# Seven norms of a two-block transformer taken token tile by token tile, with the first gate and up chunks computed in rows and turned

## The reference

```python
# first block, for l in 0, 1
h = rmsnorm(x, norm_mix_g[l])
q, k, v, f_logit, cx, cb, cc, px, gate_logit = split(h @ w_in[l])
merged = g0 * attention(q, k, v, f) @ w_attn_out + g1 * conv(cx, cb, cc) @ w_conv_out + g2 * pooling(px)
x = x + merged @ w_o[l]
h = rmsnorm(x, norm_ffn_g[l])
gt, up = split(h @ w_ffn_in[l])
x = x + (silu(gt) * up) @ w_ffn_out[l]
# second block, for i in 0, 1
h = rms_norm(x, norm_mix[i]) * (1 + scale1) + shift1
x = x + gate1 * mixer_i(h)          # i = 0: latent attention, i = 1: dilated attention
h = rms_norm(x, norm_mlp[i]) * (1 + scale2) + shift2
x = x + gate2 * (square(relu(h @ mlp_w1[i])) @ mlp_w2[i])
```

## Time and profile before

| | us |
|---|---|
| median of 3 runs | 1592.36 |
| lowest, highest | 1590.96, 1592.88 |
| profiled execution, its own time | 1587.97 |
| its span | 1586.2 |
| TensorE busy | 1539.4 (97%) |
| its weight load busy | 1391.3 (88%) |
| VectorE busy | 1126.1 (71%) |
| ScalarE busy | 819.1 (52%) |
| GpSimd busy | 132.5 (8%) |

### The profile page before, as it was taken

How to read it: one execution, slowest core, us unless ns; L and a number is a source line. 1 busy time by engine, 2 the same in 40 slices (tenths; PEclk the granted TensorE clock), 3 DMA queues, 4 the chain that set the end, 5 groups by cost and what they waited for, 6 DMA issues and landing times. The chain is left out here.

```text
span 1586.2 us, 26606 instructions
## 1 busy us (share of the span) xinstructions
PE 1539.4 (97%) x10982; PEld 1391.3 (88%) x10982; DVE 1126.1 (71%) x1437; ACT 819.1 (52%) x1089; POOL 132.5 (8%) x119
## 2 busy tenths in 40 slices
PE   7999999999999999999999999999999999999998
PEld 6999989999799999999987789998888888889997
DVE  6797678875779767877678666666878766765554
ACT  6564454344646444344468654445556555564442
POOL 2060000000123000000014000000211102000000
PEclk9999999999999999999999999999999999999999
DMA  9766376676687537676733256665877754455562
GB/s 330 261 219 211 116 256 214 213 237 245 215 265 239 187 108 254 227 234 218 230 118 101 92 188 236 229 242 170 289 268 262 256 186 160 130 163 181 191 187 79
DMA packets 224872, 325.41 MB, mean 205 GB/s; under 512 B 7944, under 2 KB 183536, under 8 KB 224752
## 3 DMA queue, kind: packets, MB, share of 16 engines
q1 hardware_dynamic: 217688, 313.00, 58.9%
q10 hardware_dynamic: 7064, 10.71, 2.0%
HBM read 314.23 MB, written 9.45 MB: 204 GB/s over the span
## 5 line engine op out<-in xcount | busy, mean ns | idle before, releaser
L1727 DVE TENSOR_TENSOR wparts<-raw,wparts 128x2048 fp32r<-128x2048 f32 (+1 forms) x240 | 545.4, 2276 | 227.6 <-ACT wparts L1229 227.4
L1229 ACT ACTIVATE wparts<-raw 128x2048 fp32r<-128x2048 f32 (+1 forms) x240 | 454.9, 1897 | 142.8 <-PE bank L555 108.3
L553 PE MATMUL bank<-hT,wparts 128*128 128x256 f32 x1728 | 494.3, 286 | 3.6 <-DVE hT L1848 2.1
L555 PE MATMUL bank<-hT,wparts 128*128 128x256 f32 x1728 | 489.1, 283 | 0.0
L554 PE MATMUL bank<-hT,wparts 128*128 128x256 f32 x1728 | 489.1, 283 | 0.0
L553 PEld LDWEIGHTS bank<-hT,wparts 128*128 128x128 f32 x1728 | 331.2, 192 | 10.4 <-issue 8.1
L554 PEld LDWEIGHTS bank<-hT,wparts 128*128 128x128 f32 x1728 | 331.5, 192 | 1.2
L555 PEld LDWEIGHTS bank<-hT,wparts 128*128 128x128 f32 x1728 | 331.4, 192 | 0.0
L553 PE MATMUL bank<-wparts,aT 128*128 128x512 f32 (+2 forms) x568 | 218.0, 384 | 0.5 <-DVE aT L1809 0.5
L553 PE MATMUL bank<-wparts,hT 128*128 128x512 f32 (+2 forms) x592 | 211.6, 357 | 4.1 <-DVE wparts L1727 1.9
L554 PE MATMUL bank<-wparts,aT 128*128 128x512 f32 (+2 forms) x568 | 213.8, 376 | 0.0
(11 more groups left out here) (285 smaller groups left out, 1487.6 us busy)
## 6 DMA issues: line engine op xcount, KB each, us to landing
raw<-in_mlp_w SPq DMA_DIRECT2D x64, 1024.0 KB, 5.7
ada_raw<-in_ada_w SPq DMA_DIRECT2D x96, 512.0 KB, 6.5
raw<-in_w_ffn_in SPq DMA_DIRECT2D x44, 1024.0 KB, 5.2
raw<-in_w_in SPq DMA_DIRECT2D x43, 1024.0 KB, 5.9
raw<-in_dil_w_in SPq DMA_DIRECT2D x64, 512.0 KB, 4.6
raw<-in_w_ffn_out SPq DMA_DIRECT2D x22, 1024.0 KB, 5.1
raw<-in_w_o SPq DMA_DIRECT2D x8, 1024.0 KB, 5.1
biasb<-head_bias ACTq DMA_DIRECT2D x16, 512.0 KB, 5.6
```

Of the source, the lines that this page charges most:

```text
L553: pe.matmul(dst, held[:, 0, :], streamed[:, 0, :], start=start, stop=False)
L555: return pe.matmul(dst, held[:, 1, :], streamed[:, 0, :], start=False, stop=stop)
L1229: act.activation(view(whi[c % SPL], c), view(raw[c % RAW], c), ACT.Copy).then_inc(s_hi, 1)
L1727: dve.tensor_tensor(view(wlo[c % SPL], c), view(raw[c % RAW], c), view(whi[c % SPL], c).bitcast(F32), ALU.subtract).then_inc(s_lo, 1)
```

## The change

- N0 to N5 and N7 go by single blocks of one token tile (128x128): TensorE transposes four or five blocks of tile 0 ahead (`turn_ahead`), then alternates one block's products with one transpose (`turn_block`, into six or five banks in turn); the same for tile 1. High and low parts are 128 wide: 16 of each instead of 8. VectorE norms tile 0 whole (`norm_first_tile`, 1024 columns), and tile 1 stays shared between the two engines. ScalarE's last square is taken between the second and the third high part, except in N0.
- GT's and M1's first chunks (`first_rows`) hold tokens and stream weights. ScalarE copies the two tiles' rows to xnf or xnp (`copy_rows`), and four transposes in the middle of the next chunk bring them into the form that was there before (`turn_rows`).
- In `mlp` the gate rows stand between the tiles of the first chunk.
- Seven second chunks (`HALVED`) have their low part written in two halves, at set places of the norm.
- The last two DN chunks go tile 0 for both, then tile 1 for both. M2 runs two M1 chunks behind instead of one. The dilated output's steps take tile 0 first. N6 keeps its form.

In N0 the order is by half chunks: blocks 0 to 3 of both tiles, then 4 to 7 of both.

```diff
-            for c in range(NF2 + 1):
+            for c in range(NF2 + 2):
                 if c < NF2:
                     chunk(("M1", i, c), kmajor(A["mlp_w1_2"][i], 256 * c, 256))
-                if c:
-                    chunk(("M2", i, c - 1), kmajor(A["mlp_w2_2"][i][256 * (c - 1):256 * c, :], 0, D))
+                if c >= 2:
+                    chunk(("M2", i, c - 2), kmajor(A["mlp_w2_2"][i][256 * (c - 2):256 * (c - 1), :], 0, D))
...
+        def turned(e):
+            if e:
+                return [(t, k) for t in range(TT) for k in range(DK)]
+            return [(t, 4 * half + k) for half in range(2) for t in range(TT) for k in range(4)]
+
+        def block_low(e, t, k):
+            return h_done[("nrm", e)] - TT * DK + turned(e).index((t, k)) + 1
...
-            project_out(*range(8, 20))
+            project_out(8, 9, 12, 13, 16, 17, 10, 11, 14, 15, 18, 19)
...
+            def turn_block(e, xn, t, k):
+                if k == 0:
+                    pe.wait_ge(s_xn, 2 * e + t + 1)
+                elif (t, k) == (1, DK // 2):
+                    pe.wait_ge(s_xn2, upper_done(e, 1))
+                b = norm_banks[turned(e).index((t, k)) % len(norm_banks)]
+                begin("a", ("nrm", e, t, k), freed_by=(s_hlo, block_low(e, t, k)), b=b)
+                end(pe.transpose(bank[b][:, 0:P], xn[:, t, P * k:P * k + P], ident[:, :]), ("nrm", e, t, k))
+
+            def lead(e):
+                return 5 if e in (1, 3, 4) else 4
+
+            def turn_ahead(e, xn, t):
+                for k in range(lead(e)):
+                    turn_block(e, xn, t, k)
+
+            def first_rows(name, w, e, xn, between=idle):
+                for t in range(TT):
+                    if t:
+                        between()
+                        turn_ahead(e, xn, 1)
+                    rows = name + ("rows", t)
+                    bk = begin("w", rows)
+                    for k in range(DK):
+                        pe.wait_ge(s_hlo, block_low(e, t, k))
+                        m = mm3(bk[:, 0:256], hT[:, :, k, P * t:P * t + P], w[:, :, k, :], k == 0, k == DK - 1)
+                        if k + lead(e) < DK:
+                            turn_block(e, xn, t, k + lead(e))
+                    end(m, rows)
+                used(name, name + ("rows", 1))
+
+            def turn_rows(name, xn):
+                for t in range(TT):
+                    emptied(pe, name + ("rows", t))
+                turn(name, lambda i, t: xn[:, t, P * i:P * i + P], 2)
+
...
+            def ffn_last_two(key, accs, nf, hid0):
+                ws = {}
+                for t in range(TT):
+                    for c in (nf - 2, nf - 1):
+                        if t == 0:
+                            ws[c] = weights((key[0], key[1], c))
+                            pe.wait_ge(s_hidlo, hid0 + c + 1)
+                        down_tile(key, c, ws[c], accs, nf, t)
 
...
+                def next_block(t, k):
+                    if l:
+                        turn_block(e, xn1, t, 4 + k)
+                    elif (t, k) == (1, 3):
+                        for t2 in range(TT):
+                            for k2 in range(4, DK):
+                                turn_block(e, xn1, t2, k2)
...
+                    if i == 0:
+                        order = None if l else [(t, 2 * kp + k) for kp in range(2) for t in range(TT) for k in range(2)]
+                        wide_half((nm, l), (nm, l, half), w, half, tiled=e, between=second_tile, amid=first_half_low,
+                                  after=next_block, order=order)
+                    elif i == 1:
...
+                        if c == 0:
+                            first_rows(("M1", i, c), w, 5 + 2 * i, xnp, lambda: gate_rows(2 * i + 1, 40, i))
...
+            def norm_high(e, at, gain):
+                for t, k in turned(e)[at]:
+                    bk = full(act, ("nrm", e, t, k))
+                    act.activation(hT_hi[:, k, P * t:P * t + P], bk[:, 0:P], ACT.Copy, scale=gain(k)).then_inc(s_hhi, 1)
+
+            def norm2_tile_high(e, at, i, which):
+                for t, k in turned(e)[at]:
+                    bk = full(act, ("nrm", e, t, k))
+                    shift, gain = mods[:, i, 24 * which + k:24 * which + k + 1], gain2[:, i, which, k:k + 1]
+                    dst = hT_hi[:, k, P * t:P * t + P]
+                    if k % 2 == 0:
+                        act.activation(dst, bk[:, 0:P], ACT.Identity, bias=shift, scale=gain).then_inc(s_hhi, 1)
+                    else:
+                        h = h32[1][:, k // 4, P * (k // 2 % 2):P * (k // 2 % 2) + P]
+                        if t:
+                            act.wait_ge(s_hlo, block_low(e, 0, k))
+                        link(act.activation(h, bk[:, 0:P], ACT.Identity, bias=shift, scale=gain))
+                        act.activation(dst, h, ACT.Copy).then_inc(s_hhi, 1)
...
+                norm_high(2 * l, slice(0, 2), gain_mix)
+                if l:
+                    norm_sums(2 * l, sq1, (3,))
+                    norm_high(2 * l, slice(2, 8), gain_mix)
+                    norm_upper(2 * l, xn1, (1,))
+                    norm_high(2 * l, slice(8, 16), gain_mix)
+                else:
+                    norm_upper(2 * l, xn1, (1,))
+                    split_half(1)
+                    split_next[0] = 1
+                    norm_high(2 * l, slice(2, 16), gain_mix)
...
+                norm_sums(2 * l + 1, sqf, (0, 1, 2))
+                split_ahead(("GT", l, 0), 1)
+                norm_high(2 * l + 1, slice(0, 2), gain_ffn)
+                norm_sums(2 * l + 1, sqf, (3,))
+                norm_high(2 * l + 1, slice(2, 8), gain_ffn)
+                norm_upper(2 * l + 1, xnf, (1,))
+                copy_rows(("GT", l, 0), xnf, 0)
+                norm_high(2 * l + 1, slice(8, 16), gain_ffn)
+                copy_rows(("GT", l, 0), xnf, 1)
...
+                norm2_tile_high(e, slice(0, 2), i, 1)
+                norm_sums(e, sqp, (3,))
+                norm2_tile_high(e, slice(2, 8), i, 1)
+                norm_upper(e, xnp, (1,))
+                copy_rows(("M1", i, 0), xnp, 0)
...
                 gate_rows(2 * i + 1, gbc2)
-                norm_upper(5 + 2 * i, xnp)
...
+            def norm_first_tile(ev, xn):
+                i = RSTD_OF[ev]
+                dve.wait_ge(s_rstd, i + 1)
+                dve.tensor_scalar(xn[:, 0, :], x[:, 0, :], rstd[:, i % 2, 0:1], None, ALU.mult).then_inc(s_xn, 1)
...
+                    tile_low(0, slice(0, 2), gain_mix)
+                    norm_lower(0, xn1, 1)
+                    tile_low(0, slice(2, 6), gain_mix)
+                    split_half(1)
+                    split_next[0] = 1
+                    tile_low(0, slice(6, 12), gain_mix)
+                else:
+                    tile_low(2, slice(0, 2), gain_mix)
+                    norm_mean(2, 1)
+                    tile_low(2, slice(2, 5), gain_mix)
+                    norm_lower(2, xn1, 1)
+                    tile_low(2, slice(5, 12), gain_mix)
+                split_halved(("Q", l, 1), 0)
+                split_halved(("Q", l, 1), 1)
+                tile_low(2 * l, slice(12, 16), gain_mix)
...
+                tile_low(2 * l + 1, slice(0, 2), gain_ffn)
+                norm_mean(2 * l + 1, 1)
+                tile_low(2 * l + 1, slice(2, 8), gain_ffn)
+                norm_lower(2 * l + 1, xnf, 1)
+                split_halved(("UP", l, 0), 0)
+                tile_low(2 * l + 1, slice(8, 16), gain_ffn)
+                split_halved(("UP", l, 0), 1)
...
+                    if q == 1:
+                        split_ahead(("LI", 0) if l else ("Q", 1, 0), 0)
+                        norm_mean(2 * l + 2, 0)
                     if q == 2:
-                        norm_mean(2 * l + 2, 0)
-                dve.wait_ge(s_bout, BOUT * (l + 1))
+                        dve.wait_ge(s_bout, BOUT * (l + 1))
+                        norm_first_tile(2 * l + 2, xnm if l else xn1)
```

More of the change, by code:

```diff
@@ L584, in _, with wide_half @@
             wide_banks = {}
-            def wide_half(name, chunk_name, w, half, first_of=None, between=idle):
+            def wide_half(name, chunk_name, w, half, first_of=None, between=idle, tiled=None, amid=idle, after=idle,
+                          order=None):
                 at = 4 * half
-                for t, k, _, _ in block_order(TT, 4, first_of and not half):
+                for t, k in order or [tk[0:2] for tk in block_order(TT, 4, first_of and not half)]:
                     if t and k == 0:
@@ L599, in wide_half @@
                         end(m, name + (t,))
+                    last = m
+                    after(t, k)
                 if half:
@@ L602, in wide_half @@
                 else:
-                    m.then_inc(s_w, 1)
+                    last.then_inc(s_w, 1)
                     ended["w"] += 1
@@ L607, in token_major @@
             def token_major(name, w, c0, nc_, a, k0, kk, toks=(0, 1), first_of=None, between=idle,
```

(50 more changed lines are left out.)

328 lines of the change are left out of this document (201 added, 127 removed).

## The result

The changed kernel takes 1619.21 us (median of four runs, 1616.19 to 1622.44) against 1591.66 for the kernel before: a ratio of 1.0177, interval 1.0158 to 1.0195, so **27.5 us slower**. Slower was forecast, but by 11.25, and 1619.2 lies outside the range. The profiled execution took 1622.44 with a span of 1620.6; against that of the kernel before (1586.2) it is 34.4 longer. Two single runs far above all others of their kernels (1627.87 of the kernel before, 8566.19 of the one with the tile form at N1 to N4 alone, further down) count as slow and are left out of the ratios.

What follows compares the result with a forecast made beforehand. TensorE, busy 97% of the span, was taken to bound the kernel. Terms 6.9 - 0.5 - 0.45 - 0.5 + 1.0 + 2.2 + 2.6 = +11.25 us gave 1603.6 us, range 1597.5 to 1610.

Steps and rivals of the forecast that it cites:

- costed at nothing: M2 one chunk later, the MO and DN reorderings and the DMA queue, all taken to add no time.
- N1 and N3: Plain norms ahead of UP and GT: 9.45 against 10.39, less 0.46 for turning rows back, -0.5 us each.
- N0: First norm, at the start: second Q chunk at 23.9 instead of 18.73, +5.2, and +1.7 for the clock.
- The heads: First layer's heads, behind the first norm: no term in the sum, 0 in the table of stages.
- N2, N4, N5, N7: Norm before the second layer's Q, then three modulated norms: -0.45, +1.0, +2.2 and +2.6 us.
- The prices of halved blocks: 128-wide parts in the norms: ScalarE's high part 0.39, modulated 0.46; VectorE's low part 0.34, modulated 0.41.
- ScalarE's pairs: Modulated norms: a pair of blocks costs ScalarE 1.02 us, bounds 0.7 and 1.25.
- The estimate from the figures of the Trainium skill: ScalarE from PSUM, 0.25 at 128 columns; by it each modulated norm about 0.8 shorter; the prediction kept to the rows.
- Gate rows "in full": N5 and N7: gate rows between the tiles, no longer under the norm's wait, cost 1.85 in full at N5.
- The overlap works: Rival: tiles hide four fifths of the norms' 19.4 of waiting; -4.75, 1587.6 us; chance 0.05.
- N0's wait is shorter: Rival: high parts at 0.2, no clock fall, modulated pairs at TensorE's pace; +6.2, 1598.6 us; chance 0.2.
- The clock falls at more norms: Rival: clock falls in N5, N7 and one other norm, 3 x 1.7; 1608.7 us; chance 0.2.

Runs made afterwards that it cites:

- the other bank: The changed kernel with GT0's turn at N1 and N3 taking a bank of the other ring, loads still late: 1609.08 us, ratio 1.0109.
- together: Changed kernel with bias loads behind UP1, GT0's turn in another ring, Q's second chunk split ahead, N5, N7, first M1 chunk and last output steps old: 1591.30 us.
- three: Changed kernel with bias loads behind UP1's chunk, GT0's turn in another ring's bank, and Q's second chunk split ahead in the first norm: 1596.06 us, ratio 1.0037.

## Why the prediction was right in its sign and wrong in its size

**The step that failed** is in "costed at nothing": "the DMA queue, which waits on low parts but has whole chunks of slack". Both halves of it are wrong. SyncE's queue waits on more than low parts: behind UP0's chunk it waits for both tiles' norm, 34.8 in two waits in the kernel before. And at this place there was no chunk of slack: GT1's weights were split 0.9 ahead of its first product (213.00, 213.87), and the later norm takes 2.8 of the request's lead. I followed the waits of the engines whose rows I had read, and took the queue for a stream of chunks.

**Left out of the same sentence, and the larger part**: the ring of banks. A chunk that becomes three jobs shifts every later job of a ring of three, and GT1 gets a bank that is drained only behind UP1's split. With the loads out of the way it alone left N1 and N3 at +3.9 where both mended give -2.6, so 6.5. With the bank mended and the loads still late they stand at +3.3, so 5.8 (and 1.5 more behind N3, as above). The two together: 14.3 + 2.6 = 16.9 in the profiles and 18.9 in the medians, more than the whole forecast, and more than the two apart, since the late split of UP1 holds back the drain that GT1 waits for.

**N0: right in mechanism, some 1.7 short.** The second chunk started at 25.13, not 23.9. The first product was at 10.58 and not 9.9, since VectorE's half of the weights waited for ScalarE's high part. And the products ran at the lower level (0.43 apart) until about 16.1, where the sum had full speed from 12.5 on: some 0.8 more. The wait is then 6.4 instead of 5.2. The clock fell as forecast: 8.6 - 6.4 = 2.2 is left for it, against 1.7 (0.50 from 25 to 29.5).

**The heads, +4.0, were forecast at nothing**, and the profile makes them a matter of chance: VectorE normed the probabilities late, TensorE waited 1.75 and 0.29, and the clock fell (0.73 in the 4 us from 103).

```profile
103.31 0.55 PE L846 MATMUL bank<-ident,P 128*128 128x128 f32 x3 [1.75 <-DVE P L2275]
```

Three of the eleven profiles taken since (the change, the other bank, and "together" above) show a piece of 1.65 to 1.75 here; it costs them +2.8 to +4.0. In the others none is over 0.74, and all eight lie within 0.7 of the kernel before at the same anchors. It goes with the arrival of the forget sums that all heads wait for: GpSimd takes them up 45.3 to 46.4 behind N0's anchor in the three, and 42.0 to 44.9 in the eight. That it is the cause is argued and not shown, and what decides the arrival stays open; the spread of 6 us between the runs of the change may be the same thing, which no run shows.

**N2, N4, N5, N7: right** to within 0.4, by their own steps; N1 and N3 too once the faults are out, by 1.0 and 0.5 better. The waits of N4, N5 and N7, read as the prediction reads them, are within 0.35 of its terms one by one (N4: 1.5, 1.2, 1.1, 0.7 and 0.6 for 1.5, 1.15, 1.1, 0.6 and 0.9). The prices of halved blocks, which no row of before had, measured in the change (groups by form):

```profile
L1446 ACT ACTIVATE hT<-bank,colA 128x128 fp32r<-128x128 f32 x64 | 19.9, 371 | 13.2 <-PE bank L696 12.4
L2058 DVE SCALAR_TENSOR_TENSOR hT<-bank,colA,hT 128x128 fp32r<-128x128 f32 x64 | 19.4, 346 | 11.3 <-PE bank L696 7.4 <-ACT hT L1446 3.0
...
L1454 ACT ACTIVATE hT<-bank,mods,gain 128x128 fp32r<-128x128 f32 x24 | 10.7, 448 | 4.9 <-PE bank L696 4.9
```

So 0.371, 0.346 and 0.448 for the 0.39, 0.34 and 0.46 taken, each from the nearest row. ScalarE's pairs at N5 came 1.09 apart (947.80, 948.89) for the 1.02. The estimate from the figures of the Trainium skill (VectorE: DVE Perf Modes, the section on the TRN2 errata), 0.25 for ScalarE from PSUM at 128 columns, is not what these rows show; the measurement decides. Gate rows "in full" was right too: hidden behind the transposes they gave 3.6 of their twice 1.95.

**The rivals.** *The overlap works* was wrong: even with every fault mended, N0, N5 and N7 cost. *N0's wait is shorter* was wrong, it was longer. *The clock falls at more norms* was right in effect and wrong in place: in the change it fell at N1 and N3, behind pieces of 6.5 and 6.05, and not at N4, N5 or N7. That it stayed up at N7 was chance. N7 has the same two waits of 1.01 and 1.16, with four transposes between them, in the six profiles with this form, and in two of them (Q's chunk split ahead, and "three") the clock fell behind them and the stage cost 4.0 and 3.9 instead of 3.0. The prediction had looked for falls at one piece of 2.63 alone; the kernel before has one behind a piece of 1.50 too (last section). "Three", and then the change:

```profile
1400.00:1404.00 4.00, 3.92 (x19) 0.57 0.01 4
```

```profile
1428.00:1432.00 4.00, 3.50 (x26) 1.00 0.01 4
```

The rule of the Trainium skill weighed there (TensorE: Matmul & The Clock Gate, Part 4), that the full clock does not engage for transposes, would have had it fall where transposes and short waits alternate with products. With both faults mended, N1's transposes and its waits, 0.58 and 0.73, kept 1.00, and N7's kept it in four profiles of six: these runs neither bear the rule out nor exclude it.

With the two faults out, the change measures +7.8 us in the medians (8.8 by the ratio) and +13.3 in the profiled executions, on which the forecast's stages were summed, against a forecast of +11.25. Of the 13.3 some 1.6 are in the latent heads, where the clock fell behind a piece of 1.61 (0.57 in the 4 us from 893.5) in this profile and not in that of the change.

## What to carry to other kernels

When a change moves when something is ready, search the whole program for every wait on that semaphore, the queue that issues the transfers included: work queued behind such a wait in order is late although it has nothing to do with it. When a step turns one job of a ring of buffers into several, count the ring on to the next product and ask which job holds the buffer it gets. Price a fault by its stage in the traces and not by the medians alone, which mix in what other stages did by chance. And take a change apart: here the form at N1 to N4 was worth 2 us, and it lay under 31 us of other parts and of two faults.

## What the hardware showed that I had not expected

The clock fell behind idle pieces much shorter than the 6.5, but not each time, and it cost less there: at N1 1.5 of work behind 2.52 and 1.4 behind 2.25, against 2.8 behind 6.49. Behind the same piece of 2.52 at N3 it did not fall. And in the latent attention all twelve profiles have a piece of 1.50 at the same place: in five of them, the kernel before among them, the granted clock in the 4 us behind it was 0.57 to 0.64, in the other seven 1.00 (0.64 from 836 to 840 in the kernel before, 1.00 from 864 to 868 in the change). What decides it no run here shows. So a single short wait has no fixed price in clock, and two profiles of one kernel can differ by more than 1 us for it.
